# A quarter of a depthwise convolution moved from TensorE to VectorE, and a layer norm's two reductions moved between later tiles

## The chip, the cores and the metric

The kernel runs on one core of one Trainium2 chip. The metric is the device time of one launch in microseconds (us).

## The reference

One decoder block on 256 tokens plus 16 meta tokens (272 rows, `D_MODEL` 1024), all in float32. A projection `w_in` gives the input of a state-space branch, the value and gate of a convolution branch, and two sets of merge gates. Cut to what matters here:

```python
c = val * sigmoid(gate)                        # 512 channels
c = depthwise_causal_conv(c, dw_w) + dw_b      # 31 taps for each channel
mu = mean(c, over the 512 channels); var = mean((c - mu)**2)
c = silu((c - mu) * rsqrt(var + eps) * ln_g + ln_b)
yb = c @ w_conv_out
ya = gelu(s5(u)); ya = (ya @ w_s5_lin) * sigmoid(ya @ w_s5_gate)
h = h + (sigmoid(gate_a) * ya + sigmoid(gate_b) * yb) @ w_out
h = h + moe(rmsnorm(h))                        # 32 experts, top 4 of 32
```

`s5` is a linear recurrence over time with complex diagonal states. The mixture of experts reads about 400 MB of weights.

## The kernel before

Each engine has its own program; semaphores tie them together. The activations lie transposed in SBUF: 128 channels on the partitions, time along the free dimension, so that 512 channels are `MT` = 4 groups of [128, 256].

**TensorE.** The order of its work in the first stage is written out by hand in `PE_ORDER` (L301 to L306): 28 tiles `z` of the projection (L1238, eight fp32 matmuls each, listed by the profile as 16 instructions), and between them pieces named in the dictionary `between`: `("in", m)` drives the recurrence's group m (L1289), `("out", m)` computes its output tile (L1302 to L1309) from the states, `("conv", m)` is the convolution of channel group m (L1324), and `("mean", 0)` is the layer norm's mean over channels by a matmul with a matrix of 1/512 (L1332). After the list come `variance()` (L1338), eight tiles of the products with `w_s5_lin` and `w_s5_gate` (L1378, called S5 tiles below), eight tiles of the product with `w_conv_out` (L1390), and the product with `w_out` (L1425). Then follow router, plan and the experts' blocks: `gate_up` (L1476), `down` (L1487).

**The convolution on TensorE.** For each group m, `conv(m)` takes 32 matmuls (64 listed) with 32x32 matrices of taps. GpSimd writes those matrices (`tap_matrices`, L527), one group at a time, and the 16 DMAs at L394 make four shifted copies of the input `cin`. ScalarE adds the bias and puts the result in `cacc[:, m, :]` (L666).

**VectorE** works through `recurrence(0)` to `recurrence(3)` (L939 to L964; the last instruction of each frees `("out", m)` through the semaphore `states`), then subtracts the mean (L995), adds epsilon to the variance (L998), computes the reciprocal root (L1000 to L1004), scales (L1005, `ln_ready`), and then merges the eight S5 tiles (`s5_merge`, L1011 and L1013) and the eight tiles of the convolution branch (L1021, L1023). `link` makes an instruction wait for the end of the one before it.

**ScalarE** empties the PSUM banks of the `z` tiles (L620; the S5 tiles wait for the last of them), and after tile z25 squares the centred values (L670) and applies `gelu` four times (L634). Then it takes the root (L684), the gates of the S5 tiles (`s5_gate`, L679, where gate k waits for merge k-2) and the four `Silu` of the convolution branch (L689).

**GpSimd**, besides the tap matrices, prepares split biases of the experts once the three loads at L409 have landed: six instructions, L541 to L546, on [96, 2048] or [32, 2048], each linked to the one before. SyncE issues the loads at L409 when `("out", 3)` is done (`y_mm`), and then the loads that follow in its program, among them `gffn` (L412), the row of weights of the second norm, which needs `early` from column 2048 on.

**SyncE** issues all weight loads in one queue. Ring slots are reloaded when `used_up` says that the tiles which read them are done. In the experts' stage each load waits for the block that last used its buffer (L450, L456).

Of the kernel before, what the change touches and what calls it, by code (L numbers as in the profile page):

```python
# [25 lines left out]
ALU = mybir.AluOpType  # L26
# [10 lines left out]
DS = D // 2  # L37
MT = DS // P
NB = 16
QB = NB // MT  # L40
# [30 lines left out]
def build(nc, T, out):  # L71
    with ExitStack() as ctx:
# [24 lines left out]
        def view(r, at, *dims, rows=P, dt=F32):  # L97
# [13 lines left out]
            if len(dims) == 4:  # L111
# [19 lines left out]
        wtap = view(ring, work + NB * NCK, TG, MT, 32)  # L131
        shifted = view(ring, work + NB * NCK + 1024, MT, MT, XW)
        prod = view(rA, 0, 2, 2, QB, SC)
# [5 lines left out]
        merged = view(late, 2 * MT * L, KT, S)  # L139
        csq = view(rE, 0, MT, S)  # L140
        lnr = view(rE, 1024, S)
# [85 lines left out]
        xs = view(rG, 780, 6, 16)  # L227
        pc = sb("pc", [P, 4, NB])
        sp_ = sb("sp_", [P, 16, NB])
        xi = sb("xi", [P, NB], I32)  # L230
# [51 lines left out]
                                                                  sem("tap_in"), sem("shifts"), sem("cw_ready"))  # L282
        scales = sem("scales")
        rows_in, bc_in, cp_ready = sem("rows_in"), sem("bc_in"), sem("cp_ready")
# [17 lines left out]
        between = {11: [("bc", 0)], 12: [("in", 0), ("k", 0)], 13: [("in", 1)], 18: [("out", 0)], 19: [("conv", 0), ("in", 2)],  # L302
                   20: [("conv", 1)], 21: [("out", 1), ("in", 3), ("conv", 2)], 23: [("conv", 3), ("out", 2)],
                   24: [("mean", 0)], 25: [("out", 3)], 26: [("gelu", 0)]}
        for z in range(2 * N_IN):
# [47 lines left out]
        def _(sp):  # L353
# [38 lines left out]
            for g in range(MT):  # L392
                for h in range(SH):
                    sp.dma_start(shifted[32 * h:32 * h + 32, :, g, :], cin[32 * g:32 * g + 32, :, h:h + XW]  # L394
                                 ).then_inc(shifts, 16)
            for n in range(N_IN - 1, N_IN + 3):
                load(n)
# [13 lines left out]
            sp.dma_start(rb, T["router_b"][0:1, :].to_broadcast([P, EXP])).then_inc(rw_in, 16)  # L411
            sp.dma_start(gffn, T["norm_ffn_g"][0:1, :].to_broadcast([P, D])).then_inc(late_in, 16)  # L412
            sp.wait_ge(states, MT)
            load_wo(0)
            sp.wait_ge(conv_mm, MT)
            for h in range(2):
# [6 lines left out]
            used_up(sp, N_IN + 1)  # L423
            first_gu(0, 0)
            used_up(sp, N_IN + 3)
            first_gu(0, 1)
# [67 lines left out]
        def _(pool):  # L494
# [30 lines left out]
            def tap_matrices(m):  # L525
# [9 lines left out]
                                    ).then_inc(glu, 1)  # L535
            for m in (1, 2, 3):
                pool.wait_ge(conv_mm, m)
                tap_matrices(m)
# [9 lines left out]

            pool.wait_ge(shifts, 16 * MT * SH)
            link(nc.gpsimd.memset(upper, 1.0))  # L550
            nc.gpsimd.affine_select(out=upper, in_=upper, compare_op=ALU.is_gt, fill=0.0, base=0,
# [29 lines left out]
        def _(act):  # L581
# [71 lines left out]
            for step, m in PE_ORDER:  # L653
                if step == "z":
                    empty_z(m)
                    if m == 5:
                        sine_tables()
                elif step == "bc":
                    empty_bc()
                elif step == "in":  # L660
                    empty_drive(m)
                elif step == "conv":
                    act.wait_ge(conv_mm, m + 1)
                    if m == 0:
                        act.wait_ge(glu, 1)
                    nc.scalar.activation(cacc[:, m, :], ps[:, 3, (m % 2) * S:(m % 2) * S + S], ACT.Identity,  # L666
                                         bias=colp[:, 12 + m:13 + m]).then_inc(conv_sb, 1)
                elif step == "gelu":
                    act.wait_ge(centred, 1)
                    nc.scalar.activation(csq, cacc, ACT.Square).then_inc(squared, 1)  # L670
                    for q in range(MT):
                        gelu(q)
# [8 lines left out]


            act.wait_ge(var_ready, 1)
            nc.scalar.activation(lnr, lnv, ACT.Sqrt).then_inc(ln_root, 1)  # L684
            for k in range(4):
                s5_gate(k)
            act.wait_ge(ln_ready, 1)
            for m in range(MT):
                nc.scalar.activation(cacc[:, m, :], cacc[:, m, :], ACT.Silu, scale=colp[:, 16 + m:17 + m],  # L689
                                     bias=colp[:, 20 + m:21 + m]).then_inc(conv_act, 1)  # L690
            for k in range(4, KT):
                s5_gate(k)
# [57 lines left out]
        def _(dve):  # L750
# [240 lines left out]
            recurrence(2)  # L991
            recurrence(3)

            dve.wait_ge(mean_mm, 1)
# [199 lines left out]
        def _(pe):  # L1194
# [134 lines left out]
            def mean():  # L1329
                pe.wait_ge(conv_sb, MT)  # L1330
                for m in range(MT):
# [10 lines left out]
            for step, n in PE_ORDER:  # L1342
# [14 lines left out]
                elif step == "out":  # L1357
                    outputs(n)
                elif step == "conv":
                    conv(n)  # L1360
                elif step == "mean":
                    mean()
            variance()

            pe.wait_ge(ya_ready, MT)
            for n in range(KT):
# [5 lines left out]
                for g in range(2):  # L1372
# [4 lines left out]
                    for k in range(MT):  # L1377
                        ins = nc.tensor.matmul(ps[:, bank(use), g * S:(g + 1) * S], w[:, k, (n % 4) * P:(n % 4) * P + P],  # L1378
                                               ya[:, k, :], start=(k == 0), stop=(k == MT - 1))
                ins.then_inc(mm, 1)  # L1380

            pe.wait_ge(conv_act, MT)
# [233 lines left out]
```

## Time and profile before

| | us |
|---|---|
| median of 3 runs (lowest, highest) | 1199.01 (1197.71, 1199.34) |
| the profiled execution, whole | 1199.63 |
| its span in the trace | 1197.6 |
| TensorE busy | 1127.9 (94%) |
| VectorE busy | 324.9 (27%) |
| ScalarE busy | 188.1 (16%) |
| GpSimd busy | 43.8 (4%) |

Some 2.0 us of the execution lie around the span. In the profile a stage can be found by its lines: projection, recurrence and convolution fill the first 149 us, the S5 and convolution products go to 191 us, `w_out`, second norm and router to about 237 us, and the experts take the rest. TensorE's granted clock is given as a share of 2.4 GHz. A busy share alone doesn't tell what ends the run; the chain of waits does.

### The profile page before, as it was taken

To read this page: it belongs to the slowest core of one execution; us is meant where nothing else is said; L and a number is where in the kernel's file an instruction comes from. 1 tells how busy PE (TensorE), PEld (TensorE's weight loads), DVE (VectorE), ACT (ScalarE), POOL (GpSimd) and SP (SyncE) were. 2 spreads that over 40 slices of the span, in tenths; PEclk is the share of its full clock that TensorE was granted. 3 is DMA by queue.
4 is the path that set the end of the run, shared out by engine and by line. 5 is a ranking of instruction groups with operands and counts; after the bars stand their busy time and mean duration, and the time that the engine had idled before them with its cause. 6 is when DMAs were issued, how large, how long until landed. Compare 5 with 4: busy or idle time off the path is not lost.

```text
span 1197.6 us, 17762 instructions
## 1 busy us (share of the span) xinstructions
PE 1127.9 (94%) x7148; PEld 532.1 (44%) x7149; DVE 324.9 (27%) x765; ACT 188.1 (16%) x279; POOL 43.8 (4%) x45
## 2 busy tenths in 40 slices
PE   8999999899999999989999998888888999999995
PEld 6887886443334333333343333333333334333332
DVE  5999462631122111111121111111111112111112
ACT  2311230411111111111111111111111111111002
POOL 1102230300000000000000000000000000000000
PEclk9999999999999999999999999999999999999998
DMA  9672593692999999997999999999999799999994
GB/s 263 216 203 94 202 386 123 242 408 100 430 429 428 429 428 428 429 428 310 414 429 428 428 428 429 429 428 429 429 429 428 334 387 429 429 427 428 428 428 177
DMA packets 57399, 436.43 MB, mean 364 GB/s; under 512 B 11056, under 2 KB 27504, under 8 KB 32704
## 3 DMA queue, kind: packets, MB, share of 16 engines
q1 hardware_dynamic: 57232, 436.02, 88.3%
q8 instruction: 16, 0.26, 0.1%
q10 hardware_dynamic: 144, 0.09, 0.0%
q14 instruction: 7, 0.06, 0.0%
HBM read 432.72 MB, written 1.05 MB: 362 GB/s over the span
## 4 chain that ended last, share of the span: by engine, by line
PE 70%; DMA 25%; ACT 2%; issue 1%; DVE 1%; ACTq 0%; SPq 0%; DVEq 0%
PE ps L1476 30%; DMA ring<-in_w_gate_up 25%; PE ps L1487 14%; PE ps L1238 8%; PE ps L1459 4%; PE ps L1450 2%; PE ps L1378 2%; PE ps L1425 2%; PE ps L1324 1%; PE ps L1509 1%; PE ps L1390 1%; ACT rD L725 1%; PE ps L1496 1%; PE ps L1289 0%; PE ps L1203 0%
## 5 line engine op out<-in xcount | busy, mean ns | idle before, releaser
L1476 PE MATMUL ps<-ring,rD 128*64 128x512 f32 x1664 | 368.1, 594 | 32.0 <-DMA ring<-in_w_gate_up 31.7
L1487 PE MATMUL ps<-ring,rD 128*64 128x512 f32 x1120 | 248.0, 595 | 16.0 <-ACT rD L725 15.9
L1476 PEld LDWEIGHTS ps<-ring,rD 128*64 128x64 f32 x1664 | 119.8, 137 | 266.0 <-issue 209.9
L1487 PEld LDWEIGHTS ps<-ring,rD 128*64 128x64 f32 x1120 | 79.8, 137 | 157.6 <-issue 157.3
L1160 DVE TENSOR_SCALAR rD<-ps 128x512 f32<-128x512 f32 x35 | 24.2, 691 | 424.3 <-PE ps L1476 424.3
L723 ACT ACTIVATE rD<-rD 128x512 f32<-128x512 f32 x35 | 22.0, 630 | 493.7 <-DVE rD L1160 493.7
L1238 PE MATMUL ps<-ring 128*128 128x256 f32 (+1 forms) x384 | 87.4, 386 | 0.0
L1086 DVE CAST rE<-rE 128x64 bf16 (+1 forms) x36 | 7.0, 195 | 294.4 <-PE ps L1476 294.1
L1238 PEld LDWEIGHTS ps<-ring 128*128 128x128 f32 x384 | 72.1, 190 | 12.7 <-issue 1.4
L1459 PE MATMUL ps<-rD,rE 64*128 64x512 f32 x288 | 71.6, 615 | 0.7 <-ACT rD L729 0.7
L1450 PEld LDWEIGHTS ps<-rE,rC 128*128 128x128 bf16 x1728 | 58.3, 99 | 27.3 <-issue 26.9
L1476 PE MATMUL ps<-late,rD 128*64 128x512 f32 x288 | 64.9, 592 | 0.0
L1476 PE MATMUL ps<-early,rD 128*64 128x512 f32 x288 | 64.9, 592 | 0.0
L1450 PE MATMUL ps<-rE,rC 128*128 128x64 bf16 x1728 | 63.5, 195 | 0.0
L729 ACT COPY rD<-ps 128x512 f32<-128x512 f32 x35 | 20.5, 585 | 243.7 <-PE ps L1487 243.7
L1459 PEld LDWEIGHTS ps<-rD,rE 64*128 64x128 f32 x288 | 24.8, 186 | 46.9 <-issue 45.4
L723 ACT ACT_TABLE_LOAD x32 | 41.1, 1283 | 6.3 <-DVEq L1123 5.7
L1476 PEld LDWEIGHTS ps<-early,rD 128*64 128x64 f32 x288 | 21.4, 137 | 40.4 <-issue 40.4
L1476 PEld LDWEIGHTS ps<-late,rD 128*64 128x64 f32 x288 | 21.2, 136 | 33.4 <-issue 30.4
L725 ACT COPY rD<-ps 128x512 f32<-128x512 f32 x35 | 20.5, 585 | 80.4 <-PE ps L1509 80.4
L1425 PE MATMUL ps<-ring,late 128*128 128x512 f32 x64 | 28.0, 593 | 0.0
L1378 PE MATMUL ps<-late,ring 128*128 128x256 f32 x128 | 27.8, 379 | 0.0
(332 smaller groups left out, 726.3 us busy)
## 6 DMA issues: line engine op xcount, KB each, us to landing
ring<-in_w_gate_up SPq DMA_DIRECT2D x96, 2048.0 KB, 20.6
ring<-in_w_down SPq DMA_DIRECT2D x64, 2048.0 KB, 24.5
late<-in_w_gate_up SPq DMA_DIRECT2D x16, 2048.0 KB, 24.4
early<-in_w_gate_up SPq DMA_DIRECT2D x16, 2048.0 KB, 28.8
ring<-in_w_in SPq DMA_DIRECT2D x14, 1024.0 KB, 7.9
ring<-in_w_out SPq DMA_DIRECT2D x4, 1024.0 KB, 17.0
ring<-late SPq DMA_DIRECT2D x16, 142.0 KB, 2.8
ring<-in_w_s_lin SPq DMA_DIRECT2D x2, 1024.0 KB, 5.0
```

Of the source, the lines that this page charges most:

```text
L723: nc.scalar.activation(sg, g1, ACT.Sigmoid, scale=ALPHA).then_inc(sg_ready, 1)
L725: nc.scalar.copy(actT, ps[:, 0, :].rearrange("p (j s) -> p j s", s=P)).then_inc(actT_ready, 1)
L729: nc.scalar.copy(ysb, ps[:, 2, :]).then_inc(y_ready, 1)
L1160: nc.vector.tensor_scalar(g1, ps[:, 0, :], LIMIT, None, ALU.min).then_inc(g1_ready, 1)
L1238: ins = nc.tensor.matmul(ps[:, z % 2, 0:L - n0], w[:, k, (z % 2) * P:(z % 2) * P + P], h[:, k, n0:L], start=(k == 0), stop=(k == KT - 1))
L1324: ins = nc.tensor.matmul(ps[32 * g:32 * g + 32, 3, (m % 2) * S:(m % 2) * S + S], wtap[:, a, g, :], shifted[:, m, g, SH * a:SH * a + S], st ...
L1378: ins = nc.tensor.matmul(ps[:, bank(use), g * S:(g + 1) * S], w[:, k, (n % 4) * P:(n % 4) * P + P], ya[:, k, :], start=(k == 0), stop=(k = ...
L1425: ins = nc.tensor.matmul(ps[:, 4 + 2 * c + h, :], merged[:, k, c * P:(c + 1) * P], w[:, k % 2, 512 * h:512 * h + 512], start=(k == 0), sto ...
L1450: ins = nc.tensor.matmul(ps[:, 3, k * BS:(k + 1) * BS], hp[:, part, c, k * P:(k + 1) * P], onehot[:, c, :], start=(c == 0 and part == 0), ...
L1459: ins = nc.tensor.matmul(ps[:, 4 + 2 * c + h, :], selT[64 * h:64 * h + 64, c * P:(c + 1) * P], ysb[64 * h:64 * h + 64, :], start=False, st ...
L1476: ins = nc.tensor.matmul(ps[64 * h:64 * h + 64, a, :], xT[:, k, :], gsl[odd][n][:, at:at + 512], start=False, stop=(k == KT - 1), skip_gro ...
L1487: ins = nc.tensor.matmul(ps[64 * h:64 * h + 64, 2, :], actT[:, k % 4, 64 * (k // 4):64 * (k // 4) + 64], dsl[odd][k // 4][:, at:at + 512], ...
```

## The change

The convolution's group 3 (channels 384 to 511) leaves TensorE. VectorE computes it after `recurrence(3)`: one `tensor_scalar` and 30 `scalar_tensor_tensor` instructions on [128, 256], one for each tap, each reading `cin` and the accumulator `cacc[:, 3, :]` and writing the accumulator back, and each linked to the one before. The taps come as [128, 31] by a DMA of single float32 elements, placed in SyncE's queue behind the load of slot `N_IN - 1`. `tap_matrices(3)` and a quarter of each shifted copy are gone.

`mean()` moves from before tile z24 to behind S5 tile 1, and now also waits for VectorE's group (`conv_dve`); `variance()` moves from before S5 tile 0 to behind S5 tile 3. ScalarE squares and takes the root between gate 1 and the `Silu`, and gates 2 to 7 come after the `Silu`. The squares lie in `early`, so `gffn`, which uses the same columns, is loaded only once `ln_ready` is set. GpSimd waits for `conv_dve` before it writes constants over the end of `cin`.

```diff
--- before.py
+++ after.py
@@ -36,6 +36,7 @@
 L = S + META
 DS = D // 2
 MT = DS // P
+PM = MT - 1
 NB = 16
 QB = NB // MT
 TAPS = 31
@@ -129,7 +130,7 @@
         kf = view(rF, 2 * QB * NCK, MT, 2, P)
         rtmp = view(rG, 0, QB, NCK)
         wtap = view(ring, work + NB * NCK, TG, MT, 32)
-        shifted = view(ring, work + NB * NCK + 1024, MT, MT, XW)
+        shifted = view(ring, work + NB * NCK + 1024, PM, MT, XW)
         prod = view(rA, 0, 2, 2, QB, SC)
         uT = view(rU, 0, MT, 2, NCK)
         cin = view(rP, 0, MT, CW)
@@ -137,7 +138,7 @@
         cacc = view(rQ, 0, MT, S)
         ya = view(rU, 0, MT, S)
         merged = view(late, 2 * MT * L, KT, S)
-        csq = view(rE, 0, MT, S)
+        csq = view(rF, 0, MT, S)
         lnr = view(rE, 1024, S)
         lnt = view(rE, 1280, S)
         lnv = view(rE, 1536, S)
@@ -226,6 +227,7 @@
         dts = view(rG, 770, 2, rows=NB)
         xs = view(rG, 780, 6, 16)
         pc = sb("pc", [P, 4, NB])
+        taps = pc.rearrange("p a b -> p (a b)")[:, 0:TAPS]
         sp_ = sb("sp_", [P, 16, NB])
         xi = sb("xi", [P, NB], I32)
         ss = sb("ss", [P, 16])
@@ -280,7 +282,7 @@
                                                       sem("final_scale"))
         taps_ready, conv_mm, conv_sb, tap_in, shifts, cw_ready = (sem("taps_ready"), sem("conv_mm"), sem("conv_sb"),
                                                                   sem("tap_in"), sem("shifts"), sem("cw_ready"))
-        scales = sem("scales")
+        scales, taps_in, conv_dve = sem("scales"), sem("taps_in"), sem("conv_dve")
         rows_in, bc_in, cp_ready = sem("rows_in"), sem("bc_in"), sem("cp_ready")
         blocks_ready, pc_tr, bdown_in, fin_in = sem("blocks_ready"), sem("pc_tr"), sem("bdown_in"), sem("fin_in")
 
@@ -300,8 +302,8 @@
 
         PE_ORDER = []
         between = {11: [("bc", 0)], 12: [("in", 0), ("k", 0)], 13: [("in", 1)], 18: [("out", 0)], 19: [("conv", 0), ("in", 2)],
-                   20: [("conv", 1)], 21: [("out", 1), ("in", 3), ("conv", 2)], 23: [("conv", 3), ("out", 2)],
-                   24: [("mean", 0)], 25: [("out", 3)], 26: [("gelu", 0)]}
+                   20: [("conv", 1)], 21: [("out", 1), ("in", 3), ("conv", 2)], 23: [("out", 2)],
+                   25: [("out", 3)], 26: [("gelu", 0)]}
         for z in range(2 * N_IN):
             PE_ORDER += between.get(z, []) + [("z", z)]
 
@@ -391,9 +393,12 @@
             sp.wait_ge(glu, 1)
             for g in range(MT):
                 for h in range(SH):
-                    sp.dma_start(shifted[32 * h:32 * h + 32, :, g, :], cin[32 * g:32 * g + 32, :, h:h + XW]
+                    sp.dma_start(shifted[32 * h:32 * h + 32, :, g, :], cin[32 * g:32 * g + 32, 0:PM, h:h + XW]
                                  ).then_inc(shifts, 16)
-            for n in range(N_IN - 1, N_IN + 3):
+            load(N_IN - 1)
+            sp.dma_start(taps, T["conv_dw_w"][0].rearrange("j o c -> (j o) c")[:, PM * P:].rearrange("j p -> p j"),
+                         allow_slow_non_contiguous=True).then_inc(taps_in, 16)
+            for n in range(N_IN, N_IN + 3):
                 load(n)
             sp.wait_ge(drive_mm, MT)
             sp.dma_start(h2[:, 0, :], T["x"][0, 0:P, :]).then_inc(xres_in, 16)
@@ -409,10 +414,9 @@
                 sp.dma_start(bgu[32 * c:32 * c + 32, :], T["b_gate_up"][0]).then_inc(bgu_in, 16)
             sp.dma_start(rw, T["router_w"][0].rearrange("(k p) e -> p k e", p=P)).then_inc(rw_in, 16)
             sp.dma_start(rb, T["router_b"][0:1, :].to_broadcast([P, EXP])).then_inc(rw_in, 16)
-            sp.dma_start(gffn, T["norm_ffn_g"][0:1, :].to_broadcast([P, D])).then_inc(late_in, 16)
             sp.wait_ge(states, MT)
             load_wo(0)
-            sp.wait_ge(conv_mm, MT)
+            sp.wait_ge(conv_mm, PM)
             for h in range(2):
                 first_dn(0, h)
             load(N_IN + 5)
@@ -422,6 +426,8 @@
             first_gu(0, 3)
             used_up(sp, N_IN + 1)
             first_gu(0, 0)
+            sp.wait_ge(ln_ready, 1)
+            sp.dma_start(gffn, T["norm_ffn_g"][0:1, :].to_broadcast([P, D])).then_inc(late_in, 16)
             used_up(sp, N_IN + 3)
             first_gu(0, 1)
             used_up(sp, N_IN + 5)
@@ -533,7 +539,7 @@
             pool.wait_ge(mm_act, 12)
             nc.gpsimd.tensor_tensor(cin[:, :, HALO:HALO + L], cin[:, :, HALO:HALO + L], cgate, ALU.mult
                                     ).then_inc(glu, 1)
-            for m in (1, 2, 3):
+            for m in range(1, PM):
                 pool.wait_ge(conv_mm, m)
                 tap_matrices(m)
 
@@ -547,6 +553,7 @@
             nc.gpsimd.engine_nop().then_inc(bias_parts, 1)
 
             pool.wait_ge(shifts, 16 * MT * SH)
+            pool.wait_ge(conv_dve, 1)
             link(nc.gpsimd.memset(upper, 1.0))
             nc.gpsimd.affine_select(out=upper, in_=upper, compare_op=ALU.is_gt, fill=0.0, base=0,
                                     pattern=[[1, P]], channel_multiplier=-1).then_inc(late_consts, 1)
@@ -666,8 +673,6 @@
                     nc.scalar.activation(cacc[:, m, :], ps[:, 3, (m % 2) * S:(m % 2) * S + S], ACT.Identity,
                                          bias=colp[:, 12 + m:13 + m]).then_inc(conv_sb, 1)
                 elif step == "gelu":
-                    act.wait_ge(centred, 1)
-                    nc.scalar.activation(csq, cacc, ACT.Square).then_inc(squared, 1)
                     for q in range(MT):
                         gelu(q)
 
@@ -680,15 +685,17 @@
                                      ).then_inc(gated, 1)
 
 
+            s5_gate(0)
+            s5_gate(1)
+            act.wait_ge(centred, 1)
+            nc.scalar.activation(csq, cacc, ACT.Square).then_inc(squared, 1)
             act.wait_ge(var_ready, 1)
             nc.scalar.activation(lnr, lnv, ACT.Sqrt).then_inc(ln_root, 1)
-            for k in range(4):
-                s5_gate(k)
             act.wait_ge(ln_ready, 1)
             for m in range(MT):
                 nc.scalar.activation(cacc[:, m, :], cacc[:, m, :], ACT.Silu, scale=colp[:, 16 + m:17 + m],
                                      bias=colp[:, 20 + m:21 + m]).then_inc(conv_act, 1)
-            for k in range(4, KT):
+            for k in range(2, KT):
                 s5_gate(k)
 
             act.wait_ge(bias_parts, 1)
@@ -991,6 +998,16 @@
             recurrence(2)
             recurrence(3)
 
+            dve.wait_ge(taps_in, 16)
+            dve.wait_ge(glu, 1)
+            last = cacc[:, PM, :]
+            link(nc.vector.tensor_scalar(last, cin[:, PM, 0:S], taps[:, 0:1], colp[:, 12 + PM:13 + PM], ALU.mult, ALU.add))
+            for j in range(1, TAPS):
+                ins = nc.vector.scalar_tensor_tensor(last, cin[:, PM, j:j + S], taps[:, j:j + 1], last, ALU.mult, ALU.add)
+                if j < TAPS - 1:
+                    link(ins)
+            ins.then_inc(conv_dve, 1)
+
             dve.wait_ge(mean_mm, 1)
             nc.vector.tensor_tensor(cacc, cacc, ps[:, 3:4, 0:S].to_broadcast([P, MT, S]), ALU.subtract
                                     ).then_inc(centred, 1)
@@ -1327,7 +1344,8 @@
                 ins.then_inc(conv_mm, 1)
 
             def mean():
-                pe.wait_ge(conv_sb, MT)
+                pe.wait_ge(conv_sb, PM)
+                pe.wait_ge(conv_dve, 1)
                 for m in range(MT):
                     ins = nc.tensor.matmul(ps[:, 3, 0:S], invc[:, :], cacc[:, m, :], start=(m == 0), stop=(m == MT - 1))
                 ins.then_inc(mean_mm, 1)
@@ -1358,9 +1376,6 @@
                     outputs(n)
                 elif step == "conv":
                     conv(n)
-                elif step == "mean":
-                    mean()
-            variance()
 
             pe.wait_ge(ya_ready, MT)
             for n in range(KT):
@@ -1378,6 +1393,10 @@
                         ins = nc.tensor.matmul(ps[:, bank(use), g * S:(g + 1) * S], w[:, k, (n % 4) * P:(n % 4) * P + P],
                                                ya[:, k, :], start=(k == 0), stop=(k == MT - 1))
                 ins.then_inc(mm, 1)
+                if n == 1:
+                    mean()
+                if n == 3:
+                    variance()
 
             pe.wait_ge(conv_act, MT)
             for n in range(KT):
```

## Rows read from the trace of the kernel before

**Rows 1.** Page, part 4: shares of the chain that ended last.
```profile
PE 70%; DMA 25%; ACT 2%; issue 1%; DVE 1%; ACTq 0%; SPq 0%; DVEq 0%
```

**Rows 2.** Chain of waits in order of time: start us, us, what.
```profile
121.01 3.59 PE ps L1324 x64
...
130.11 1.73 PE ps L1332 x8
...
135.29 0.43 PE ps L1302 x2
...
136.95 10.56 PE ps L1238 x48
147.51 1.73 PE ps L1338 x8
149.24 27.63 PE ps L1378 x128
176.87 13.81 PE ps L1390 x64
```

**Rows 3.** By stretch: us, busy PE, PEld, DVE, ACT, POOL, clock, DMA share, GB/s.
```profile
280.00:290.00 10.00, 9.40 (x88) 4.58 (x86) 3.19 (x8) 1.78 (x3) 0.00 (x0) 1.00 0.01 2
```

**Rows 4.** VectorE in order of time: start us, us, instruction, idle before.
```profile
114.49 2.22 DVE L959 TENSOR_TENSOR ring<-early,rD 128x512 f32<-128x512 f32 x1
...
130.61 0.69 DVE L964 TENSOR_TENSOR ring<-ring 128x512 f32<-128x512 f32 x1
131.94 1.22 DVE L995 TENSOR_TENSOR late<-late,ps 128x1024 f32<-128x1024 f32 x1 [0.64 <-PE ps L1332]
149.28 0.42 DVE L998 TENSOR_SCALAR rE<-ps 128x256 f32<-128x256 f32 x1 [16.11 <-PE ps L1338]
150.18 1.75 DVE L1000 RECIPROCAL rE<-rE 128x256 f32<-128x256 f32 x1 [0.48 <-ACT rE L684]
151.97 3.18 DVE L1001 TENSOR_TENSOR rE<-rE 128x256 f32<-128x256 f32 x1
155.19 2.00 DVE L1002 TENSOR_TENSOR rE<-rE 128x256 f32<-128x256 f32 x1
...
159.12 0.43 DVE L1004 TENSOR_TENSOR rE<-rE 128x256 f32<-128x256 f32 x1
...
216.13 0.86 DVE L1070 SCALAR_TENSOR_TENSOR rE<-rE 128x32 f32<-128x32 f32 x1
```

**Rows 5.** GpSimd in order of time, columns as in rows 4.
```profile
114.02 2.14 POOL L527 TENSOR_TENSOR ring<-late,cw 128x1024 f32<-128x1024 f32 x1 [7.82 <-PE ps L1324]
142.75 1.89 POOL L541 CAST rW<-rD 96x2048 bf16<-96x2048 f32 x1 [26.59 <-DMA rD<-in_b_gate_up]
...
150.80 4.07 POOL L544 TENSOR_TENSOR rD<-rD 96x2048 f32<-96x2048 f32 x1
154.93 1.96 POOL L545 COPY rW<-rD 32x2048 bf16<-32x2048 bf16 x1
156.96 1.97 POOL L546 CAST rW<-rD 32x2048 bf16<-32x2048 f32 x1
```

**Rows 6.** Line 792: durations ns min/median/max, first and last start us, form.
```profile
L792 DVE SCALAR_TENSOR_TENSOR rD<-late,rD x3: 591/591/591, 36.5 to 37.8; 128x416 f32<-128x416 f32 x3
```

**Rows 7.** SyncE's queue in order of time.
```profile
74.08 0.61 SPq L360 DMA_DIRECT2D ring<-in_w_in  x1
```

**Rows 8.** DMA issues: count, KB, us from issue to landing.
```profile
early<-in_ssm_b_re SPq DMA_DIRECT2D x1, 128.0 KB, 10.8
```

**Rows 9.** ScalarE in order of time.
```profile
147.55 0.38 ACT L620 ACTIVATE rC<-ps 128x256 f32<-128x256 f32 x1 [1.34 <-PE ps L1238]
```

**Rows 10.** TensorE in order of time, with the idle time before it.
```profile
231.63 0.18 PE L1542 MATMUL ps<-rE,late 128*128 128x32 bf16 x1 [3.03 <-DVE rE L1073]
```

**Rows 11.** By 1 us stretch; columns as in rows 3.
```profile
234.00:235.00 1.00, 1.00 (x23) 1.00 (x21) 0.00 (x0) 0.00 (x0) 0.00 (x0) 0.50 1.18 508
...
237.00:238.00 1.00, 0.95 (x6) 0.38 (x8) 0.54 (x4) 0.00 (x0) 0.00 (x0) 0.99 1.12 475
```

## The prediction

> **What bounds the kernel now.** I read the chain that ended last first: 70% TensorE, 25% DMA, VectorE 1% [rows 1]. So I look for the stretch that the change touches and ask whether TensorE has any gap there. In the chain in order of time each piece starts where the last one ended: the last projection tiles end at 147.51 us, the variance at 149.24, the S5 tiles at 176.87, the `w_conv_out` tiles at 190.68 [rows 2]. TensorE never waits there, so a microsecond taken from or added to its program is a microsecond for everything behind.
>
> Does that reach the end, where the experts' weights stream? From 280 to 290 us the DMA moved 2 GB/s at a share of 0.01 while TensorE was busy 9.40 of 10 us [rows 3]: the queue is full of loads that wait for a buffer which TensorE has not released. The stream that ends the run is thus started by TensorE at a time that moves with the first stage. I carry every shift through one to one.
>
> **What TensorE loses and gains.** `conv(3)` goes: 64 listed matmuls, 3.59 us [rows 2]. The mean (1.73) and the variance (1.73) are moved, not removed. Up to z27 two of these three pieces lie ahead in the old order (3.59 and the mean's 1.73), so `("out", 3)`, at 135.29 before, comes up at 129.97, and ends at 136.95 - 5.32 = 131.63; z27, which ended at 147.51, ends at 142.19.
>
> **Are the states ready at 129.97?** VectorE's last instruction of `recurrence(3)` ended at 130.61 + 0.69 = 131.30 [rows 4], 1.3 us too late. But `recurrence(2)` contains an L959 of 2.22 us on [128, 512], where L964 on the same shape takes 0.69 [rows 4]. GpSimd's `tap_matrices(3)` ran from 114.02 to 116.16 [rows 5]; L959 began at 114.49 and ended at 116.71, so it did its work once GpSimd was through. That GpSimd instruction goes, VectorE gains 1.53 us, and the states are there at 129.77, just in time. If the gain doesn't come, TensorE waits 1.3 us here, but that delay would be covered by the longer wait below.
>
> **The new work on VectorE.** 31 linked instructions on [128, 256]. The form is in the trace at 416 columns: 591 ns [rows 6]. Between 256 columns (L1004, 0.43 us) and 512 (L964, 0.69) a column costs 1.0 ns [rows 4], so at 256 I get 591 - 160 x 1.0 = 0.43 us. Linked instructions follow at 0.04 us (L1000 ends at 151.93, L1001 starts at 151.97 [rows 4]), hence 0.465 us each and 14.4 us in all. From 129.8 they would end at 144.2. The mean, behind S5 tile 1, comes up on TensorE at 142.19 + about 0.5 (below) + 2 tiles of 27.63 / 8 = 3.45 [rows 2], at 149.6. By this count VectorE has 5.4 us to spare, and the change would be a gain.
>
> **But GpSimd works in that stretch.** Its six bias instructions (L541 to L546) ran from 142.75 to 158.93, released by the load at L409 [rows 5], 5.8 us after `("out", 3)` had ended at 136.95. With `("out", 3)` ending at 131.63 they start at 137.45, in the middle of the taps. What VectorE got from them before is in the same rows: L1001, on [128, 256], took 3.18 us instead of 0.43 and ended at 155.15, which is 0.28 after the end of L544 (150.80 + 4.07 = 154.87); L1002 took 2.00 and ended at 157.19, 0.30 after L545's end at 156.89 [rows 4, 5]. So a VectorE instruction with two inputs in SBUF stands until the GpSimd instruction is over, and each of these lets one through. The form of the taps does so too: L1070, a `scalar_tensor_tensor` on 32 columns only, took 0.86 us [rows 4], while GpSimd was in L576.
>
> The Trainium skill says the same as a rule, and it speaks against this change: SBUF — State Buffer, "Who interferes with whom", tells that a VectorE instruction with two SBUF inputs contends with a GpSimd one that reads SBUF, and that whoever has the shared ports first keeps them for its whole instruction. The trace agrees (3.18 against 0.43 us). By that section's other half, that issue order decides, VectorE's row of taps could hold GpSimd off instead; rival (a) below is worked out for that.
>
> Now the sum. From 129.81 at 0.465 us, 16 taps are done by 137.25 and the 17th ends at 137.7, where GpSimd's first instruction gets in. Its six take 158.93 - 142.75 = 16.2 us, and each of the five later ones may wait for the tap let in before it: 0.08 us by L546 against L541 (1.97 and 1.89 [rows 5]), at most the 0.28 that such a tap works. I take 0.15: GpSimd ends at 137.7 + 16.2 + 0.75 = 154.6, the 23rd tap at 154.9, and the other 8 take 3.7 us: `conv_dve` at 158.6. TensorE stands at the mean from 149.6 to 158.6, some 9 us.
>
> **Behind the stall.** In TensorE's queue behind the mean stand S5 tiles 2 to 7, the variance and all that follows: mean to 160.4, tiles 2 and 3 (6.91) to 167.3, variance to 169.0, tiles 4 to 7 (13.81) to 182.8, `w_conv_out` (13.81) to 196.6, against 190.68 [rows 2]: 5.9 us late. Is anything later than that? The squares need the centring (1.22 [rows 4]) and about 1 us on ScalarE; both end near 163, before 167.3. From the variance to the reciprocal was 0.9 us (149.28 to 150.18), the reciprocal takes 1.75, then L1001 to L1004 without GpSimd about 4 x 0.46 and the scaling 1.22 [rows 4]: `ln_ready` at 174.7, the first bank free at 175.2. Tile 6 comes up at 175.9, so it just isn't kept waiting; GpSimd's remaining constants are over by then. `Silu` and six gates end before 182.8 or in step with the tiles. Moving these costs nothing as long as that 0.7 us of margin holds.
>
> **Small edits.** The taps' DMA has 31 x 128 = 3968 runs of one element. The nearest row is the load of `ssm_b_re`, 2048 runs of 16 elements, 10.8 us to landing [rows 8]; times 1.94, 21 us. It goes out behind the load issued at 74.08 [rows 7], and is wanted at 129.8. Behind it in SyncE's queue are the S5 weights, wanted at 142: no cost; even twice the estimate would be held by the slack. `gffn` goes out after `ln_ready`, about 175, behind 5 MB of other loads, and is wanted by the second norm beyond 205: no cost. S5 tile 0 waits for ScalarE to empty z27 (0.38 us, begun right at the tile's end [rows 9]); the variance used to cover that. Bare, it is 0.5 us, which the stall at the mean hides here. `gelu` no longer stands behind the squares: no cost. The quarter less of the shifted copies was not waited for.
>
> **TensorE's clock.** The trace shows one fall: after a gap of 3.03 us and a second one shortly after [rows 10], the clock was granted at 0.50 of 2.4 GHz, the lower level, around 234 us, and was back at 0.99 by 237 [rows 11]. Some 3.2 us of work at half speed cost 1.6 us. A gap of 9 us is three times as long. The price lies between 0 (no fall) and about 3.4 us (twice that stretch of work at 1.2 GHz); I take 1.8, near the row.
>
> The Trainium skill, TensorE: Matmul & The Clock Gate, "What's actually happening", says that the low clock is the default state and that activity releases it; by that the fall is nearly sure here, and its price is of the size of the row's.
>
> **Sum.** 1199.63 (the profiled execution) + 5.9 + 1.8 = 1207.4. That execution lay 0.6 above the median, so for the median 1206.8.
>
> **Rivals.** (a) VectorE isn't held up, or it is GpSimd that stands. For it: the taps are a dense row, 0.04 us between two, and GpSimd has to find its way in. Against it: L1001, L1002 and L959. Then the mean doesn't wait, and TensorE saves 3.59 less the 0.5 at tile 0: 3.1 us, 1195.9. It decides if `conv_dve` is set before 149.6. (b) Part of it: GpSimd starts late, or more than one tap gets through at each change. Two instead of one would take 6 taps, 2.8 us, off the tail; only a GpSimd start past 143 would bring the time to within 2 us of before. Time 1198 to 1201. (c) Worse: the tap load is late (it would have to take over 55 us, against an estimate of 21), or the layer norm's chain keeps tile 6 waiting, as its margin is 0.7 us: 1210 to 1216. (d) The change does what it says in every case; only its price is open.
>
> **How the numbers follow.** The forecast (a stall of 8 to 10 us at the mean) has a chance of 0.80; its own bounds are `conv_dve` 1 us either way and the clock's 0 to 3.4 us, so 1203.4 to 1209.6. Rival (a) 0.09, (b) 0.05, (c) 0.06. The range 1201 to 1211 takes in the forecast's bounds and the near sides of (b) and (c). About 0.2% (2.4 us) is what a measurement of this kernel can tell from no change. Faster 0.09, same 0.05, slower 0.86.
>
> **What would show it.** In the profile after: L1324 with 192 matmuls instead of 256; `states` of group 3 near 129.8; 31 instructions of 0.43 us at VectorE, of which some six last 1.9 to 4.1 us, each ending about 0.28 after a GpSimd one; an idle time of about 9 us before the mean's first matmul; a granted clock of 0.5 behind it. If all 31 are short and the mean doesn't wait, the blocking was misread, and the kernel is faster. If the idle time is there but the end moves by less, the one-to-one carry is wrong.

## The result, and the profile after

The changed kernel takes 1210.32 us (median of 4, 1208.09 to 1211.26) against 1199.17 us (median of 4, 1197.71 to 1201.8) before: a ratio of 1.0083, 95% interval 1.0072 to 1.0095. At 1199.17 us that is 10.0 us slower (8.6 to 11.4), and the medians lie 11.2 us apart; forecast was 7.8. One execution of a kernel further down (the one with the bias instructions behind the taps) took 1323.78 us at a mean clock of 0.847; it is in that kernel's median and not in its ratio. In the profiled executions the span grew from 1197.6 to 1207.4 us.

VectorE around the taps, in the chain of waits of the changed kernel (start us, us, what); L1006 is one tap:

```profile
136.47 0.50 DVE late L1006
136.96 0.02 issue
136.99 2.10 DVE late L1006
...
139.12 4.18 DVE late L1006
...
143.32 2.00 DVE late L1006
...
145.35 4.18 DVE late L1006
...
149.56 2.00 DVE late L1006
...
151.59 2.00 DVE late L1006
...
153.62 0.49 DVE late L1006
```

The first taps last 0.50 us, six in the middle 2.1 or 2.0 and 4.18, then they are short again. They don't differ in shape. What ran beside them, GpSimd in order of time:

```profile
136.91 1.89 POOL L547 CAST rW<-rD 96x2048 bf16<-96x2048 f32 x1 [31.82 <-DMA rD<-in_b_gate_up]
138.88 4.12 POOL L548 TENSOR_TENSOR rD<-rD,rW 96x2048 f32<-96x2048 f32 x1
143.07 1.97 POOL L549 CAST rD<-rD 96x2048 bf16<-96x2048 f32 x1
145.12 4.12 POOL L550 TENSOR_TENSOR rD<-rD 96x2048 f32<-96x2048 f32 x1
149.30 1.97 POOL L551 COPY rW<-rD 32x2048 bf16<-32x2048 bf16 x1
151.34 1.97 POOL L552 CAST rW<-rD 32x2048 bf16<-32x2048 f32 x1
```

Each long tap ends shortly after a GpSimd instruction does: L547 at 138.80 and the tap at 139.09, L548 at 143.00 and the tap at 143.30. L547 started 6.3 us after `("out", 3)` ended at 130.61, half a microsecond more than the same instruction had taken before [rows 2, 5].

TensorE in order of time, with the idle time before it:

```profile
130.61 10.63 PE L1255 MATMUL ps<-ring 128*128 128x256 f32 x48
141.75 7.14 PE L1393 MATMUL ps<-late,ring 128*128 128x256 f32 x32 [0.52 <-issue]
158.41 3.75 PE L1350 MATMUL ps<-late,invc 128*128 128x256 f32 x8 [9.51 <-DVE late L1006]
161.96 7.43 PE L1393 MATMUL ps<-late,ring 128*128 128x256 f32 x32
169.22 1.89 PE L1356 MATMUL ps<-early,invc 128*128 128x256 f32 x8
170.95 13.98 PE L1393 MATMUL ps<-late,ring 128*128 128x256 f32 x64
184.76 13.98 PE L1409 MATMUL ps<-late,ring 128*128 128x256 f32 x64
```

It had finished S5 tile 1 and stood 9.51 us at the mean for the last tap, which ended at 158.28. The `w_conv_out` tiles follow at 184.93 by the chain of waits, instead of 176.87 [rows 2]. The mean's eight matmuls took 3.75 us where they had taken 1.73 [rows 2], because of the clock. Busy time by stretch (us; PE, PEld, DVE, ACT, POOL; granted clock; DMA share; GB/s):

```profile
149.00:152.00 3.00, 0.00 (x0) 0.00 (x0) 2.93 (x3) 0.32 (x1) 2.87 (x3) 1.00 1.05 405
152.00:153.00 1.00, 0.00 (x0) 0.00 (x0) 1.00 (x1) 0.00 (x0) 1.00 (x1) 0.72 1.06 420
153.00:158.00 5.00, 0.00 (x0) 0.00 (x0) 4.68 (x10) 0.00 (x0) 0.30 (x1) 0.50 1.02 408
158.00:162.00 4.00, 3.59 (x9) 2.90 (x10) 0.26 (x1) 0.00 (x0) 1.23 (x7) 0.50 1.08 452
162.00:163.00 1.00, 1.00 (x5) 0.85 (x4) 0.80 (x1) 0.00 (x0) 0.00 (x0) 0.66 0.92 393
163.00:170.00 7.00, 7.00 (x34) 6.17 (x33) 0.42 (x1) 2.34 (x2) 0.00 (x0) 1.00 0.14 61
```

The clock was still granted in full for the first three microseconds of the gap, fell to 0.50 (1.2 GHz) within it, and was back at 1.00 some four microseconds after the work resumed.

One correction before spans are compared. The profiled execution of the changed kernel was 1.1 us ahead at `conv(2)`, before anything of the change had happened on TensorE. The lead isn't the change's doing: it is there at projection tiles that run before the two programs differ (25.70 us against 26.83), and the kernel before with the useless matmuls of the last experiment, which come after 220 us, starts the same tiles at 25.83. The first line is of the kernel before, the second of the changed one:

```profile
110.24 3.66 PE L1324 MATMUL ps<-ring 128*32 128x256 f32 x64
...
109.14 3.66 PE L1341 MATMUL ps<-ring 128*32 128x256 f32 x64
```

So the stretch up to the end of the `w_conv_out` tiles cost 198.74 + 1.10 - 190.68 = 9.2 us.

### The profile page after: what moved, and what is told of

It is laid out like the page before. It is cut to its first block, busy times and chain, and to the rows that moved or that the text cites. A ratio compares the mean times of both kernels' runs of the same rounds, so it can differ in the third digit from the quotient of the medians.

```text
span 1207.4 us, 17664 instructions
## 1 busy us (share of the span) xinstructions
PE 1126.1 (93%) x7084; PEld 530.3 (44%) x7085; DVE 344.8 (29%) x796; ACT 186.4 (15%) x277; POOL 41.5 (3%) x44
## 4 chain that ended last, share of the span: by engine, by line
PE 57%; DMA 27%; DVE 11%; issue 2%; ACT 2%; ACTq 0%; SPq 0%; DVEq 0%
PE ps L1495 29%; DMA ring<-in_w_gate_up 27%; PE ps L1506 13%; PE ps L1478 3%; DVE late L1006 2%; PE ps L1469 2%; PE ps L1444 2%; PE ps L1393 2%; PE ps L1255 1%; PE ps L1409 1%; PE ps L1528 1%; ACT rD L732 1%; DVE early L956 1%; PE ps L1515 1%; DVE ring L939 0%
## 5 line engine op out<-in xcount | busy, mean ns | idle before, releaser
L1006 DVE SCALAR_TENSOR_TENSOR late<-late,pc 128x256 f32<-128x256 f32 x30 | 28.1, 935 | 1.1
```

Of the source, the lines that this page charges most:

```text
L1006: ins = nc.vector.scalar_tensor_tensor(last, cin[:, PM, j:j + S], taps[:, j:j + 1], last, ALU.mult, ALU.add)
```

## Experiments

The set asks four things: is it GpSimd that holds up the taps, do the new places of mean and variance cost anything, what does the clock add, and does the whole loss come from this stretch. All ratios are to the kernel before on the same chip.

**The changed kernel again**, as a reference for the others.

> The changed kernel once more, as the yardstick of this set. Both theories: about 1.008 times the kernel before (+10 us), an idle time of 9 to 10 us before the mean, tap instructions of 0.49 us with six of 2.0 to 4.2 us.

Measured: 1210.26 us against 1199.84, ratio 1.0094 (1.0074 to 1.0114). Its idle time before the mean was 9.41 us.

**GpSimd's bias instructions behind the taps.**

```diff
+            pool.wait_ge(conv_dve, 1)
             pool.wait_ge(bgu_in, 16 * 3)
             link(nc.gpsimd.tensor_copy(bp, bgu))
```

> GpSimd's six bias instructions wait for the last tap. Blocking theory (the taps stand behind GpSimd's instructions, and TensorE behind the taps): all 31 taps short, the last one done near 144.8 us, no idle time before the mean (TensorE comes up at 148.9), and the run 3.1 us shorter than the kernel before: about 1196, 13 us less than the changed kernel. Rival, order: if the moved mean and variance and the newly bare waits were what cost, the stall would go but 5 us or more would stay: 1201 or above. Rival, one-to-one: if part of the 10 us came from the experts' stage, that part stays.

Measured: 1195.94 us against 1199.84, ratio 0.9975 (0.9962 to 0.9987), 3.0 us faster than the kernel before and some 14 us faster than the changed one. The 30 taps of L1007 (VectorE, one line's durations in ns, min/median/max) and TensorE around the mean:

```profile
L1007 DVE SCALAR_TENSOR_TENSOR late<-late,pc x30: 483/485/486, 129.6 to 144.7; 128x256 f32<-128x256 f32 x30
...
142.22 7.15 PE L1394 MATMUL ps<-late,ring 128*128 128x256 f32 x32 [0.52 <-issue]
149.20 1.89 PE L1351 MATMUL ps<-late,invc 128*128 128x256 f32 x8
```

All taps last 0.485 us, the last ends at 145.2, and there is no gap before the mean. One added wait takes back the whole loss and leaves the gain that rival (a) of the prediction had worked out (3.1 us). So GpSimd's six instructions beside the taps are the cause, and within the interval nothing of the 10 us was left in the experts' stage.

**The new order without the new work.** Group 3 of the convolution back on TensorE, its tap matrices and shifted copies back, the taps' load gone; mean, variance, squares, root, gates and `gffn` as in the changed kernel.

```diff
-                   20: [("conv", 1)], 21: [("out", 1), ("in", 3), ("conv", 2)], 23: [("out", 2)],
+                   20: [("conv", 1)], 21: [("out", 1), ("in", 3), ("conv", 2)], 23: [("conv", 3), ("out", 2)],
...
-                pe.wait_ge(conv_sb, PM)
-                pe.wait_ge(conv_dve, 1)
+                pe.wait_ge(conv_sb, MT)
```

> The convolution's group 3 stays on TensorE as before; mean, variance, squares, root, gates and the gffn load are placed as in the changed kernel. Blocking theory: the new places cost only the bare wait for z27, 0.5 us: 1199.5 to 1200. Rival, order: a large part of the 10 us, 1204 or above.

Measured: 1198.97 against 1199.84, ratio 0.9997 (0.9985 to 1.001). The bare wait is there in its trace, 0.52 us before S5 tile 0, but a measurement can't tell it from no change. The rival on order falls.

**GpSimd only writes.** The six bias instructions become fills, which leaves the experts' biases out.

```diff
-            link(nc.gpsimd.tensor_copy(bp, bgu))
-            link(nc.gpsimd.tensor_tensor(bgu, bgu, bp, ALU.subtract))
...
+            for _ in range(8):
+                link(nc.gpsimd.memset(bp, 0.0))
```

> The changed kernel with the six bias instructions replaced by eight fills of the same tile, which GpSimd only writes (2.05 us each by the rate of its other fills, 16 us in all); the experts' biases are thereby left out. If GpSimd's reads are what holds the taps up: all taps at 0.49 us, the last done near 144.8. If it is any GpSimd work on SBUF: the taps still stretch to 2 us while a fill runs, and the last ends past 155.

Measured: 1197.77 us in one run, not compared, as its output is another one. GpSimd in order of time, and the taps of this kernel (durations in ns, min/median/max, first and last start):

```profile
138.36 14.81 POOL L548 MEMSET rW<- 96x2048 bf16 x8 [31.98 <-DMA rD<-in_b_gate_up]
...
L1002 DVE SCALAR_TENSOR_TENSOR late<-late,pc x30: 485/485/485, 130.5 to 145.6; 128x256 f32<-128x256 f32 x30
```

The fills took 14.81 us in all (16 expected). GpSimd was at work from 138.36 to 153.17, across half of the taps, and not one of them was longer than 485 ns. So it isn't GpSimd at work on SBUF that holds a tap up: where it only writes, both run; where it reads, the tap waits. The Trainium skill, SBUF — State Buffer, "Who interferes with whom", states just this distinction for a VectorE instruction with two SBUF inputs, and both runs agree with it (0.485 us beside fills, 2.0 to 4.2 beside casts and subtractions). That one engine keeps the ports for its whole instruction the section says of VectorE's two-port modes; for two SBUF inputs the trace of the changed kernel shows it.

Two SBUF inputs are not the only form that was held. First the kernel before, while GpSimd's L546 ran to 158.93; then the same instruction with GpSimd past its reads, and a subtraction of a PSUM bank from SBUF beside two of GpSimd's reading instructions (147.25 to 153.28), both in the kernel with the moved bias instructions:

```profile
157.21 1.87 DVE L1003 TENSOR_SCALAR rE<-rE 128x256 f32<-128x256 f32 x1
...
163.37 0.29 DVE L1021 TENSOR_SCALAR rE<-rE 128x256 f32<-128x256 f32 x1
151.12 1.22 DVE L1013 TENSOR_TENSOR late<-late,ps 128x1024 f32<-128x1024 f32 x1 [5.90 <-PE ps L1351]
```

The `tensor_scalar` has one SBUF input and two constants, and took 1.87 us for 0.29. The subtraction, with one input in SBUF and one in PSUM, took the same 1.22 us as before with GpSimd idle [rows 4].

**A busy TensorE at the stall.** Twenty matmuls whose result is overwritten, in front of the mean.

```diff
             def mean():
                 pe.wait_ge(conv_sb, PM)
+                for r in range(20):
+                    nc.tensor.matmul(ps[:, 3, 0:S], invc[:, :], cacc[:, r % PM, :], start=True, stop=True)
```

> The changed kernel, with 20 matmuls of no use (results overwritten) in front of the mean, 8.6 us of work in the time that TensorE otherwise idles. If the lower clock behind the stall is a cost of its own, the granted clock stays at 1.0 and the run is 2.0 to 2.3 us shorter than the changed kernel: about 1208, 1.0065 times the kernel before. If the clock costs nothing there: no change, 1.008.

Measured: 1206.39 against 1199.64, ratio 1.0055 (1.0041 to 1.0068). TensorE in order of time:

```profile
148.93 8.80 PE L1349 MATMUL ps<-late,invc 128*128 128x256 f32 x40
158.54 1.99 PE L1352 MATMUL ps<-late,invc 128*128 128x256 f32 x8 [0.82 <-DVE late L1006]
...
182.82 13.98 PE L1411 MATMUL ps<-late,ring 128*128 128x256 f32 x64
```

The granted clock stays at 1.00 (148 to 170 us). The mean lasts 1.8 us again, and from the mean's start at 158.54 to the `w_conv_out` tiles at 182.82 it is 24.28 us, where the changed kernel takes 26.35 (158.41 to 184.76): 2.1 us for the clock. The timed gain is somewhat larger, but its interval and that of the changed kernel leave 0.5 to 6.5 us, so the trace is the better measure. (The whole spans of these two profiles can't be compared: this one stood at 0.50 for 13.6 us around the router, the changed kernel's for 3.4.)

**The mean two tiles later, the variance one**, in the changed kernel otherwise as it is.

```diff
-                if n == 1:
+                if n == 3:
                     mean()
-                if n == 3:
+                if n == 4:
                     variance()
```

> The changed kernel, with the mean behind S5 tile 3 and the variance behind tile 4. The wait for the taps falls to about 2.8 us, but the layer norm's chain on VectorE then ends near 171, and tile 6, which needs a bank that VectorE empties after it, waits some 2.8 us: 6.5 us less than the changed kernel, about 1203.5. If the wait simply goes: 9 us less.

Measured: 1202.63 against 1199.64, ratio 1.0032 (1.0019 to 1.0045), 3.8 us above the kernel before. TensorE in order of time:

```profile
142.23 14.05 PE L1393 MATMUL ps<-late,ring 128*128 128x256 f32 x64 [0.52 <-issue]
158.94 1.97 PE L1350 MATMUL ps<-late,invc 128*128 128x256 f32 x8 [2.65 <-DVE late L1006]
...
172.19 7.17 PE L1393 MATMUL ps<-late,ring 128*128 128x256 f32 x32 [2.65 <-DVEq L1029]
```

The one stall of 9.5 us has become two of 2.65: at the mean, and before S5 tile 6, which waits for VectorE to empty its bank behind the layer norm. The clock stays at 1.00 (150 to 180 us). Hiding the wait behind more tiles only uncovers the next thing on VectorE.

**Constants in place of the column of taps.** As with the moved bias instructions, with 0.125 for each tap and no bias, so this group's convolution is a different one and the experts' blocks with it.

```diff
-                ins = nc.vector.scalar_tensor_tensor(last, cin[:, PM, j:j + S], taps[:, j:j + 1], last, ALU.mult, ALU.add)
+                ins = nc.vector.scalar_tensor_tensor(last, cin[:, PM, j:j + S], 0.125, last, ALU.mult, ALU.add)
```

> As pool_later, but each tap's factor is a constant in the instruction instead of a column of SBUF, so the convolution of this group is another one, and the experts' blocks with it; read only the taps' durations. If the column costs the 0.06 us by which the taps were longer than predicted: 0.425 us each instead of 0.485. If not, 0.485.

Measured (VectorE, durations in ns, min/median/max, first and last start):

```profile
L1007 DVE SCALAR_TENSOR_TENSOR late<-late x30: 424/426/428, 129.0 to 142.4; 128x256 f32<-128x256 f32 x30
```

426 ns, 59 less than with the column, all of what the taps were longer than forecast. Its total time (1213.42 us) is of other blocks of experts and is not compared.

**A kernel that beats both.** The moved bias instructions, and S5 tiles 0 to 3 without the wait for tile z27.

```diff
-                if n < 4:
-                    emptied(pe, S5_USE - 1)
-                else:
+                if n >= 4:
                     emptied(pe, use - 6)
```

> As pool_later, and S5 tiles 0 to 3 no longer wait for ScalarE to empty projection tile z27 (their banks are others). The wait of 0.5 us before S5 tile 0 should go: 0.5 us less than pool_later, about 1195.6. If TensorE waits there for another reason, no change.

Measured: 1196.67 against 1199.84, ratio 0.9976 (0.9966 to 0.9986); faster than both kernels, but not than the one with the moved bias instructions alone (0.9975). The gap of 0.52 us before S5 tile 0 is gone from its trace, and yet its span (1196.1) is 3.1 us longer than that kernel's (1193.0). By stretches, first two lines of the kernel with the moved bias instructions, then one of this; last the router's first matmul in the former, with the gap before it:

```profile
222.00:225.00 3.00, 3.00 (x5) 1.27 (x4) 2.90 (x9) 1.70 (x3) 1.85 (x2) 0.50 0.69 295
230.00:237.00 7.00, 6.55 (x78) 3.39 (x76) 1.06 (x7) 0.58 (x1) 0.00 (x0) 1.00 1.01 422
...
229.00:237.00 8.00, 7.65 (x66) 4.02 (x64) 0.77 (x5) 0.58 (x1) 0.00 (x0) 0.50 1.00 421
...
228.31 0.18 PE L1562 MATMUL ps<-rE,late 128*128 128x32 bf16 x1 [1.34 <-DVE rE L1091]
```

Both profiles have a fall to 0.50 of some 3.4 us ahead of the router, from about 222 and 221 us; the only gap shortly before it is one of 0.90 us. The fall stretched eight matmuls of TensorE from 3.68 to 5.38 us, and so the router's gaps are 1.34 and 1.09 us in both, not 3.03 and 1.09 as before [rows 10]. Behind these gaps the kernel with the moved bias instructions kept the full clock; this one stood at 0.50 for about ten microseconds more, from 228 to 238. This led to three more runs.

**Useless matmuls in the router's gaps.**

```diff
+            def filler(k):
+                for _ in range(k):
+                    nc.tensor.matmul(ps[:, 3, 0:P], ident[:, :], invc[:, :], start=True, stop=True)
+
             pe.wait_ge(late_consts, 7)
+            filler(13)
             pe.wait_ge(masks, 2)
...
+            filler(4)
             pe.wait_ge(onehot_ready, 1)
```

> As best, and TensorE does 17 matmuls of no use while it waits for the router's choice (13 before the counting, 4 behind it), 3.9 us of work in gaps of 3.0 and 1.1 us. If the fall of the clock behind these gaps is what cost best 3 us against pool_later in their profiles: granted clock at 1.0 from 200 to 240 us, and 2 to 5 us less than best, 1192 to 1194.5. If the clock costs nothing there: no change, or up to 0.5 us more.

> The kernel best once more, as the yardstick for best_warm: 0.9976 times the kernel before. Its profile shows how much of the stretch from 216 to 240 us lies at the lower clock this time; if that hangs on the moment at which the gaps fall, it differs from the first profile (about 13 us at 0.5).

> The kernel before with the same 17 useless matmuls in the router's gaps. If the clock's fall there (3.2 us at 0.5 in the profile) is a cost of the kernel before as well: 1.6 us less at least, 1197.5 or below. If not: 1199.2 to 1199.7.

Measured on one chip, the kernel before at 1200.17: with the matmuls 1194.81, ratio 0.9953 (0.994 to 0.9966); without them 1196.68, 0.9962 (0.995 to 0.9974); the kernel before with them 1198.64, 0.9983 (0.9974 to 0.9991). By stretches, first the fast kernel with the matmuls, then the kernel before with them:

```profile
226.00:232.00 6.00, 5.49 (x84) 4.37 (x84) 3.27 (x17) 1.75 (x3) 1.12 (x2) 1.00 0.68 254
232.00:240.00 8.00, 8.00 (x41) 2.75 (x37) 2.09 (x11) 1.28 (x1) 0.00 (x0) 1.00 0.98 390
...
221.00:222.00 1.00, 0.27 (x3) 0.03 (x1) 0.62 (x1) 1.00 (x2) 0.00 (x0) 1.00 0.76 180
225.00:228.00 3.00, 3.00 (x5) 1.35 (x4) 2.90 (x8) 1.68 (x3) 2.48 (x3) 0.50 0.51 218
234.00:240.00 6.00, 5.55 (x71) 2.77 (x69) 0.77 (x5) 0.59 (x1) 0.00 (x0) 1.00 1.01 429
```

The fast kernel keeps the clock throughout, as expected. Its time is 1.9 us below that of the same kernel without the matmuls (2 to 5 expected), and as the two intervals overlap, only the medians speak for that. The fast kernel without them, profiled once more, had one fall and not two, from about 231 to 234, behind gaps of 3.22 and 1.09 us:

```profile
231.00:234.00 3.00, 2.83 (x52) 2.56 (x49) 0.13 (x1) 0.45 (x1) 0.00 (x0) 0.50 1.02 429
```

So one and the same program stood at 0.50 for 13.7 us in one profile and for 3.4 in another.

The kernel before gained 2.0 us by the ratio (1.1 to 3.1), where 1.6 or more was expected. Its profile doesn't show why. With the matmuls the clock fell ahead of the router, at 225 to 228, after a gap of 0.90 us that ended at 222.2, and stayed up at the router; but that is 3.4 us at 0.50, as much as without them. The single executions say more. Of the 17 of the kernel before on this chip, seven had a mean clock of 0.992 to 0.994 and took 1201.64 to 1202.5 us, the other ten 0.995 or 0.996 and 1199.44 to 1200.59. All eleven with the matmuls had 0.996 or 0.997 and took 1197.98 to 1199.23. A part of the gain is thus that the longer executions no longer occur. That they are those with a long fall at the router is likely, as the profile with 13.7 us at 0.50 also had a mean clock of 0.992, but no profile of such an execution of the kernel before was taken.

## Why the prediction was right

The mechanism and its place were as forecast; the sum came out 1.5 us short in the stretch (7.7 of 9.2): 0.8 by the length of a tap, 0.1 by the step from the last tap to the mean's start (0.14 us, taken as nothing), 0.5 by the clock. The measured median, 1210.32, lies in the range of 1201 to 1211, but above the forecast's own upper bound of 1209.6. (By the terms given for them the forecast's bounds are 1204.0 and 1209.4, and twice 1.6 us is 3.2, not 3.4.) That the range held with 0.7 us to spare is in part luck.

**Carry to the end.** Right. The added wait gave back the stretch's loss and the whole run's with it. The two profiles leave 1.7 us more (9.8 - 9.2 + 1.1 of the head start) in the router and experts' stage. About 1 us of it is the last load before the end, 25.17 us in one trace and 24.15 in the other; the changed kernel run again had 24.21 there, and only 0.7 us left by the same sum. The rest was not traced further.

**The states.** Right: without `tap_matrices(3)` the last instruction of `recurrence(3)` ended at 128.69, and with the 1.1 us of the head start that is the forecast 129.8; TensorE didn't wait.

**The length of a tap.** Mis-sized: 0.465 us forecast, 0.52 measured (0.50 and 0.02 between two). I took the `scalar_tensor_tensor` at L792, whose factor is a constant; the taps' factor is a column of SBUF, which costs 59 ns more, as the run with constants showed. L975 in the trace of before has the right form (346 ns at 128 columns); scaled by 1.0 ns a column it gives 0.47 us, or 0.51 with the link. It was the nearer row, and I passed it over. The price of a mis-sized tap: nine taps, not eight, were left behind GpSimd's last instruction, at 0.52 each 4.7 us instead of 3.7, less the 0.2 by which GpSimd was early, so 0.8 us.

**The blocking.** Right in kind and size: GpSimd's start after `("out", 3)` (5.8 us forecast, 6.3 measured; the three loads held SyncE for 2.25 us where it had been 1.27, which may be why), one tap let through by each instruction, the forecast 154.6 for GpSimd's end against 153.31 + 1.1 = 154.4. That end is so close because two errors cancel: GpSimd began 0.3 us later than forecast (136.91 + 1.1 = 138.0 against 137.7), and its six instructions took 16.4 us, not 16.95. They gave way by less than I took, at most 0.06 to 0.08 us each (L548 4.12 for 4.06, L549 1.97 for 1.89). The last tap was forecast at 158.6 and ended at 158.28 + 1.1 = 159.4.

**Behind the stall.** Right: TensorE waited for nothing between the mean and the end of the `w_conv_out` tiles; the bare wait before S5 tile 0 (0.5 us forecast, 0.52 measured) was hidden by the stall. The margin of 0.7 us at tile 6 held.

**The clock.** Mis-sized a little: 1.8 us forecast. From the chain, mean and tiles 2 and 3 took 158.41 to 169.39, 11.0 us, instead of 8.6: 2.3 us; by the run with a busy TensorE 2.1.

**Small edits.** The taps' load landed 9.3 us after its issue (21 estimated) and held SyncE for 0.7 us; no cost, as forecast.

**The rivals.** (a), VectorE not held up, is what the added wait made of the kernel, and its time came out as worked out for it. (b) and (c) did not occur: no second tap got through at any change, the taps' load was early, and tile 6 didn't wait. The measured median lies in the span of times given for (c), without its mechanism.

## What to carry to other kernels

Before work goes to VectorE as a row of instructions with two SBUF inputs (or of `tensor_scalar`s like L1003), look in the trace for what GpSimd reads in that stretch, and for the stretch into which it will move once TensorE is faster: the same six instructions that had cost nothing before came to lie in the middle of the taps. With GpSimd out of the way the last tap ended at 145.2 us and the mean came up at 149.2, so VectorE had 4 us to spare (5.4 forecast); what the change needed was one wait on GpSimd, whose results were still ready (at 161.3 us) before the first engine asked for them (at 174). When a later consumer is pushed back to hide a stall, follow what else its engine has to deliver.

## What the runs showed that I had not expected

The clock's fall around the router is fixed neither to the kernel nor to the length of a gap. Gaps of 3.0 and 1.1 us were followed by 0.50 for 3.4 us in the kernel before [rows 11]. Gaps of 1.34 and 1.09 us were followed by no fall in one kernel and by ten microseconds at 0.50 in another whose program differs there in nothing, and that other kernel, profiled twice, had 13.7 and 3.4 us at 0.50 in all. Two kernels that are 0.5 us apart in work can so differ by 3 us in a profile the other way round. What decides whether and where the fall comes was not settled. That 17 useless matmuls in these gaps take 2.0 us off the kernel before is shown by its interval; how they do it is not.
